# The order of token positions on the partitions of a one-hot list, in a routed-expert step

## What is computed

```
scores = sigmoid(t @ router_w);  sel = scores + router_bias
... the 8 best experts of a token, within its 4 best groups of 8 -> idx, weights w -> gates (token, expert)
hid    = silu(einsum('td,edf->tef', t, exp_w_gate)) * einsum('td,edf->tef', t, exp_w_up)
hid    = hid * gates[:, :, None]
routed = einsum('tef,efd->td', hid, exp_w_down)        # D = 1024, FF = 256, 64 experts
```

## Time and profile before

| what | value |
|---|---|
| median of three runs | 1271.95 us |
| the profiled execution | 1271.95 us, its span 1270.1 us |
| PE busy | 1121.3 us (88%) |
| DVE busy | 1069.1 us (84%) |
| ACT busy | 802.5 us (63%) |
| POOL busy | 222.8 us (18%) |
| DMA, q1 (weights and other plain loads) | 294.06 MB, 63.5% of 16 engines' span |
| DMA, q0 (issued by POOL) | 31.75 MB in 20144 packets, 6.9% |

### The profile page before, as it was taken

How to read it: one execution, slowest core, us unless ns; L and a number is a source line. 1 busy time by engine, 2 the same in 40 slices (tenths; PEclk the granted TensorE clock), 3 DMA queues, 4 the chain that set the end, 5 groups by cost and what they waited for, 6 DMA issues and landing times.

```text
span 1270.1 us, 16915 instructions
## 1 busy us (share of the span) xinstructions
PE 1121.3 (88%) x5670; PEld 937.8 (74%) x5670; DVE 1069.1 (84%) x1454; ACT 802.5 (63%) x1005; POOL 222.8 (18%) x154
## 2 busy tenths in 40 slices
PE   4999999779989985788999999999999999999700
PEld 1799999645558974777888888888888888888600
DVE  5769999999976727557999999999999999999458
ACT  6543334667775413336888888888888888888401
POOL 1000000300000010011423232332332333232100
PEclk9999999899999998598999999999999999999955
DMA  9663556334446155337999999999999999999296
GB/s 349 188 162 100 151 158 164 101 99 145 156 130 202 67 213 205 120 133 291 370 362 378 378 362 377 374 368 354 363 349 353 365 380 357 363 379 353 85 356 239
DMA packets 124876, 330.22 MB, mean 260 GB/s; under 512 B 26200, under 2 KB 67831, under 8 KB 99863
## 3 DMA queue, kind: packets, MB, share of 16 engines
q1 hardware_dynamic: 101856, 294.06, 63.5%
q0 software_dynamic: 20144, 31.75, 6.9%
q10 hardware_dynamic: 2824, 3.74, 0.9%
HBM read 328.22 MB, written 43.24 MB: 292 GB/s over the span
## 4 chain that ended last, share of the span: by engine, by line
PE 61%; DVE 19%; DMA 13%; ACT 3%; issue 3%; SPq 1%; ACTq 0%; POOLq 0%; DVEq 0%
PE bank L1575 18%; PE bank L1577 17%; PE bank L1576 17%; DMA raw<-in_exp_w_down_dram 8%; PE bank L1585 5%; DVE lgu L1460 3%; DVE lo L1065 3%; DVE zb L1163 2%; DVE lo L1466 2%; DMA raw<-in_w_out_dram 1%; DVE slots L1529 1%; ACT hi L977 1%; DMA slots<-sh_d 1%; DVE mx L1238 1%; DMA raw<-in_mod_w_dram 1%
## 5 line engine op out<-in xcount | busy, mean ns | idle before, releaser
L1460 DVE TENSOR_TENSOR lgu<-raw,hgu 128x2048 fp32r<-128x2048 f32 x128 | 291.9, 2281 | 6.0 <-ACT hgu L970 6.0
L970 ACT ACTIVATE hgu<-raw 128x2048 fp32r<-128x2048 f32 x128 | 245.1, 1915 | 5.0 <-DMA sh_d<-shy 5.0
L1575 PE MATMUL bank<-hgu,xgh 128*128 128x512 f32 x512 | 206.5, 403 | 2.9 <-DVE lgu L1460 2.8
L1577 PE MATMUL bank<-hgu,xgl 128*128 128x512 f32 x512 | 201.2, 393 | 0.0
L1576 PE MATMUL bank<-lgu,xgh 128*128 128x512 f32 x512 | 199.9, 390 | 0.0
L1466 DVE TENSOR_TENSOR lo<-raw,hi 128x2048 fp32r<-128x2048 f32 x64 | 147.4, 2304 | 34.4 <-ACT hi L977 34.1
L1065 DVE TENSOR_TENSOR lo<-raw,hi 128x2048 fp32r<-128x2048 f32 (+3 forms) x61 | 133.1, 2185 | 50.0 <-ACT hi L742 49.9
L709 POOL DMA_INDIRECT y_d<-ys,ixt x64 | 129.5, 2023 | 55.1 <-ACT ys L1008 35.3
L977 ACT ACTIVATE hi<-raw 128x2048 fp32r<-128x2048 f32 x64 | 122.9, 1920 | 24.7 <-DMA raw<-in_exp_w_down_dram 24.6
L742 ACT ACTIVATE hi<-raw 128x2048 fp32r<-128x2048 f32 (+3 forms) x61 | 111.2, 1828 | 40.3 <-DMA raw<-in_w_out_dram 21.9
L1163 DVE SCALAR_TENSOR_TENSOR zb<-zb,cwt 128x400 f32<-128x400 f32 x240 | 135.3, 627 | 0.6
(11 more groups left out here) (288 smaller groups left out, 2141.0 us busy)
## 6 DMA issues: line engine op xcount, KB each, us to landing
raw<-in_exp_w_gate_dram SPq DMA_DIRECT2D x64, 1024.0 KB, 11.6
raw<-in_exp_w_up_dram SPq DMA_DIRECT2D x64, 1024.0 KB, 7.9
raw<-in_exp_w_down_dram SPq DMA_DIRECT2D x64, 1024.0 KB, 10.6
raw<-in_mod_w_dram SPq DMA_DIRECT2D x20, 1024.0 KB, 5.2
slots<-y_d SPq DMA_DIRECT2D x6, 2048.0 KB, 15.5
raw<-in_w_in_dram SPq DMA_DIRECT2D x16, 512.0 KB, 5.4
raw<-in_w_in_dram SPq DMA_DIRECT2D x8, 1024.0 KB, 5.3
mraw<-in_mod_w_dram SPq DMA_DIRECT2D x4, 1024.0 KB, 15.8
```

Of the source, the lines that this page charges most:

```text
L970: act.activation(hgu[k % 2][:, :, w, :], src, ACT.Copy).then_inc(ghi_done, 1)
L1460: dve.tensor_tensor(lgu[k % 2][:, :, w, :], src, hgu[k % 2][:, :, w, :].bitcast(F32), ALU.subtract).then_inc(glo_done, 1)
L1575: pe.matmul(out, ah, bh, start=first, stop=False)
L1577: return pe.matmul(out, al, bh, start=False, stop=last)
```

## The change

The table `slot` is replaced by `iota`, of the same size and at the same place in the constants. Before, column m held `m % 8 * 16 + m // 8`: places 0 to 15 of a list lay on partitions 0, 8, 16, ..., 120, places 16 to 31 on partitions 1, 9, ..., 121, and so on. Now column m holds m: place q lies on partition q, and an expert with n tokens uses partitions 0 to n - 1. Nothing else reads the table. No instruction is added, removed or moved on any engine, no semaphore or buffer changes, and the same rows are fetched and written for each expert; they pass through other partitions of `xg` and `ys`.

```
-             "slot": np.broadcast_to((i % 8 * 16 + i // 8)[None, :], (P, P))}
+             "iota": np.broadcast_to(i[None, :], (P, P))}
...
-        ident, before, ones, slot = (cst_of(n) for n in ("ident", "before", "ones", "slot"))
+        ident, before, ones, iota = (cst_of(n) for n in ("ident", "before", "ones", "iota"))
...
-                dve.tensor_tensor(oh[k % 2][:, :, :], slot.unsqueeze(1).to_broadcast([P, NT, P]),
+                dve.tensor_tensor(oh[k % 2][:, :, :], iota.unsqueeze(1).to_broadcast([P, NT, P]),
                                   pos3[:, :, one].to_broadcast([P, NT, P]), ALU.is_equal).then_inc(oh_done, 1)
```

## The result

The changed kernel takes 1286.91 us (median of four runs, 1285.67 to 1290.27), the kernel before 1272.82 us in the same comparison: ratio 1.0112 [1.0087, 1.0138], 14.1 us slower where 2.7 to 3.5 were forecast. The sign was right, the size wrong by a factor of four to five. The execution whose trace is read here took 1288.13 us with a span of 1286.3 us.

The account below looks back on a forecast made before the run. PE was taken to set the pace at 9.66 us a step, with DMA nearly as full. Terms 2.2 + 0.3 + 1.0 = 3.5 us on 1271.95 us gave 1275.5 us, range 1270 to 1287 us.

Parts of the forecast that it names:

- What bounds the kernel: Expert steps: PE sets the pace at 9.66 us a step; DMA is slower by 1% from 623 to 780 us.
- the lead: Work DVE and ACT had done ahead in the first steps; 1.4 us of it eaten by 780 us.
- Which engines carry the rows: Gathers and scatters: each DMA engine serves two groups of four partitions 32 apart; a row costs 0.160 us.
- The 43 extra rows: Fullest DMA engine over 64 experts: 393 rows before, 436 after, 43 more each way.
- Rivals 2 and 3: Engines pair partitions at 16: near 1290 us, chance 0.05; consecutive partitions spread better: 1271.3 us, chance 0.07.
- Stretch of 623 to 780 us, +2.2 us and 0.3 ahead of it: 14 more rows on the fullest engine cost PE 2.2 us; extra rows in earlier steps cost 0.3 us.
- From 780 us on, +1 us: Later steps: DMA's mean 9.56 us stays below PE's 9.66; only runs of full experts cost, +1 us.
- 7.50 us: DMA time a step for weights and all else: 9.766 us less 14.1 rows at 0.16 us.
- Rival 1: Full engine has no room anywhere: 1277.5 to 1285.8 us, up to 13.8 us slower, chance 0.27.
- the fixed part: DMA time a step apart from rows, taken as 7.50 us; from about 7.6 us the first rival decides.
- What would show it: Signs: down loads landing in 13 us or more, ACT's wait over 17.4 us, PE 2 us below 139.86, step elsewhere 9.66.

Follow-up runs that it names:

- e1: Changed kernel with the table spreading each list's places over all 16 DMA engines: 1271.2 us, 0.9986 of the kernel before.
- e3: Changed kernel with the table packing places, eight to an engine, so engine 0 gets 8 rows of every expert: 1315.19 us, 1.0332 of the kernel before.
- e2: Changed kernel with the table spreading the first 64 places over engines 0 to 7 (partitions 0 to 63): 1271.77 us, 0.9986 of the kernel before.
- e9: Kernel before, without one of the three products of the down projection (4 of 36 matmuls a step): 1264.7 us, 0.9916 of the kernel before.
- e10: Changed kernel without one of the three products of the down projection: 1287.77 us, 1.0111 of the kernel before.
- e15: Changed kernel, same table, with SP issuing the down weights ahead of the up weights: 1272.47 us, 0.9989 of the kernel before.
- e13: Changed kernel with engine 0 getting six rows of every list, the other 15 engines sharing the rest: 1312.48 us, 1.0308 of the kernel before.
- The mirror: Changed kernel with the table reversed, place q on partition 127 - q: 1277.34 us, 1.0028 of the kernel before.
- e7: Changed kernel with engine 0 getting eight rows of every list, the other 15 engines sharing the rest: 1345.14 us, 1.0580 of the kernel before.

## Why the prediction was wrong

*What bounds the kernel.* Right: PE at 9.66 us a step, DMA just behind it, the lead used up at 780 us. The loop of the down weights was even read out piece by piece, and that was the place to stop: its fixed 7 us and PE's 19.3 us for two steps give a limit of 12.4 us for the landing, and the trace of before had that landing at 12 to 13 us in the first stretch. The 9.766 us a step of that stretch is half a turn of this loop (136.72 us are seven turns of 19.53), not the work of an engine.

*Which engines carry the rows.* Right, by e1 to e3; and a scatter of 34 rows alone now takes six rows in line, as forecast (rounds of 8, 8, 8, 8, 1 and 1). The 43 extra rows are counted from it. Rivals 2 and 3 fall: by the one e2 would be the slower table, by the other the change a gain. The steps are counted one expert too late (the loads from 623.57 us on go with gathers of experts 8 to 21, not 9 to 22): 13 more rows in the stretch, not 14, and nothing hangs on it.

*Stretch of 623 to 780 us, +2.2 us and 0.3 ahead of it.* The same 14 steps took 136.72 us and now take 141.01 (623.70 to 764.71), 4.3 more, and 0.1 ahead of them. PE pays here, as forecast, but twice as much; the 2.2 us came from the price of a row below.

*From 780 us on, +1 us.* This is the step that failed: measured 9.9 us over the 41 steps up to expert 59 and 2.6 us behind them. The sum took the mean load of the fullest engine in a step (7.50 us and 0.16 a row, 9.56 in all) and set it against PE's 9.66. Two things were wrong in that. The sizes: a row was priced at 0.16 us from a scatter that ran alone, and e9 and e10 show 0.33 us or more for 1.5 rows, 0.22 each, as what they cost the loop; the room was 0.20 us a step, not 0.34; and the 7.50 us was worked out of 9.766, the pace of the loop, as if that were an engine's work. And the kind: an engine's load was taken for its deadline. The limit is on the landing of one load, and the waits behind it repeat every two steps; e15 keeps the load and moves the issue 2.3 us ahead, and nothing is lost.

*Rival 1* named the size, up to 13.8 us if every extra row counts, with 0.27. It decided on the fixed part alone, from 7.6 us on; e9 gives 9.46 - 11.4 x 0.16 = 7.64, so by its own criterion it was the case, though that criterion gave 5.5 to 7 us; that its outer limit comes near the 14.1 us measured is chance: 86 rows of 0.16 us aren't what the loss is made of, for with the same rows e15 has none. Its reason, an engine with no room anywhere, is not what e15 shows. The argument against it, only 6.1 us of waits in the long stretch, says nothing on how near a hidden wait is to showing: waits are a threshold effect, and the distance to the threshold (10.6 of 12.4 us) had to be weighed against what the landing would gain (2.2 us).

*What would show it.* Loads of 13 us or more between 640 and 780 us: the first in the chain took 15.03 us, but the median there is 12.9. ACT's waits beyond 17.4 us: 26.6. PE below 139.86 us by 2: it has 137.16. PE's step of 9.66 elsewhere: no, 9.88.

*What stays open.* Why the landing grows faster than the rows. From before to after it grew 2.2 us (10.6 to 12.8) for 0.24 to 0.33 us more work in a step, and in e13 one engine with six rows among light ones lands at 13.8 us where eight engines with six to eight rows each (before) land at 10.6. Neither the count of rows nor the engine's number tells this, and the spread of 1.0028 to 1.0112 among equal counts belongs to it. Nor is a packet of weights the same everywhere: before, from 780 to 1170 us, q1 moves 127.32 MB in 84.4% of 16 engines' time, 0.34 us for 8 KB in the mean. With 24 of them and 11.4 rows of 0.16 us an engine would need 10.0 us a step, and a step took 9.64; so on the full engines the packets were shorter than the mean, or their times overlap. A queue that never empties before the next issue would make landings grow so, and the holes of e13 show one engine whose queue hasn't emptied when all others have; no run here separates this from packets that take longer.

## What to carry to other kernels

When a load sits in a chain of waits, write its loop down: buffers x step, minus the fixed pieces between landing and the next issue, is the longest landing that stays hidden. A change that only lengthens the landing is free while all loads stay below that, and costs each step the excess divided by the number of buffers above it. (The mirror, with a median of 11.5 us in the long stretch, lost 4 us all the same.) An engine's mean load doesn't answer that question, and the mean share over 16 DMA engines can fall while DMA becomes the limit. Ask first what the next issue is queued behind: here the down load stood behind a load with time to spare, and with the table of after to swap the two in SP's order was worth as much as the whole placing of the rows.

## What the runs showed that I had not expected

- A transfer of 128 rows of which 54 are real is as long as its fullest DMA engine's rows, and which partitions the real rows lie on decides that; skipped rows still pass as small packets of about 8 ns.
- The cost of a busy DMA engine depends on the others: 512 rows on it cost 42 us when its neighbours are full as well (e3) and 72 us when they are light (e7); 384 rows cost 39 us among light engines (e13), and 393 nothing among engines as full (before).
- The same 64 loads of 1024 KB land in 12.8 or 8.2 us by their place in SP's order alone (after, e15), with equal bytes and the same table.
